# First chunk over 512 tokens beside the loads, spare weight buffers for one output chunk, and small PE steps put later

## What is computed

```python
# first block
h = rmsnorm(x, norm_pre)
pool_u, pool_gate, q, k, v, attn_gate = split(h @ w_in)
pool_out = pool_mixer(pool_u, pool_w, pool_scale) * silu(pool_gate)   # trailing means over 2, 4, 8, 16 tokens
attn_out = sliding_window_attention(q, k, v, sinks) * silu(attn_gate)
x = x + rmsnorm(concat(pool_out, attn_out) @ w_out, norm_post)
# second block
h = rms_norm(x, norm1)            # two attentions and two gates from h @ w_in_2
merged = g_a * (o_a @ w_branch_a) + g_b * (o_b @ w_branch_b)
x = x + merged @ w_out_2
x = x + square(relu(rms_norm(x, norm2) @ w_up)) @ w_down
return rms_norm(x, final_norm)
```

## Time and profile before

| what | value |
|---|---|
| median of 3 runs | 1962.76 us (1958.78 to 1962.78) |
| time of the profiled execution | 1964.96 us |
| its span, first to last instruction | 1963.1 us |
| PE busy, share of the span | 98% |
| DVE, ACT, POOL busy | 48%, 32%, 48% |
| mean granted TensorE clock | 0.995 |
| share of PE in the chain that ended last | 91% |

### The profile page before, as it was taken

The page is one execution under the profiler, slowest core; times in us unless marked ns, Lnnn a source line. Parts: engine busy times, 40 slices in busy tenths (PEclk is TensorE's granted clock), DMA queues, the critical chain, the costliest instruction groups (busy, mean ns, idle before and its releaser), DMA issues.

```text
span 1963.1 us, 27207 instructions
## 1 busy us (share of the span) xinstructions
PE 1924.7 (98%) x9792; PEld 1621.6 (83%) x9792; DVE 946.7 (48%) x1733; ACT 625.2 (32%) x1175; POOL 939.2 (48%) x806
## 2 busy tenths in 40 slices
PE   7999999999999999999999999999999999999998
PEld 6778887888888988888888887878888888888886
DVE  5535664677554544453411116654444444444455
ACT  5025555546444544454300003331111111111133
POOL 3442237622122222112344444486777767777784
PEclk9999999999999999999999999999999999999999
DMA  4311013231111111100111113121121111211103
GB/s 129 103 48 32 29 40 96 81 131 42 36 41 46 26 49 43 44 22 23 33 48 48 48 48 129 54 74 43 43 67 55 51 43 44 71 53 49 54 29 133
DMA packets 147217, 111.98 MB, mean 57 GB/s; under 512 B 11400, under 2 KB 139920, under 8 KB 147104
## 3 DMA queue, kind: packets, MB, share of 16 engines
q1 hardware_dynamic: 134880, 91.77, 16.0%
q10 hardware_dynamic: 12224, 18.70, 3.1%
HBM read 102.00 MB, written 11.59 MB: 58 GB/s over the span
## 4 chain that ended last, share of the span: by engine, by line
PE 91%; DVE 4%; issue 1%; POOL 1%; ACT 1%; DMA 1%; SPq 0%; DVEq 0%; POOLq 0%; ACTq 0%
PE ps L811 7%; PE ps L812 7%; PE ps L813 7%; PE ps L954 7%; PE ps L828 6%; PE ps L829 5%; PE ps L830 5%; PE ps L1171 5%; PE ps L1172 5%; PE ps L1170 5%; PE ps L1131 5%; PE ps L1132 5%; PE ps L1133 5%; PE ps L943 4%; PE ps L929 2%; PE ps L924 2%
## 5 line engine op out<-in xcount | busy, mean ns | idle before, releaser
L667 POOL TENSOR_TENSOR w_hi<-raw,ones 128x512 fp32r<-128x512 f32 x146 | 159.7, 1094 | 797.3 <-PE ps L830 498.3
L2367 DVE TENSOR_TENSOR X<-ps,X 128x1024 f32<-128x1024 f32 x112 | 137.2, 1225 | 205.4 <-PE ps L1172 205.4
L811 PE MATMUL ps<-h_hi,w_hi 128*128 128x512 f32 x544 | 215.1, 395 | 6.0 <-DVE h_lo L1746 3.4
L812 PE MATMUL ps<-h_lo,w_hi 128*128 128x512 f32 x544 | 212.8, 391 | 0.0
L813 PE MATMUL ps<-h_hi,w_lo 128*128 128x512 f32 x544 | 212.7, 391 | 0.0
L671 POOL TENSOR_TENSOR w_lo<-raw,w_hi 128x512 fp32r<-128x512 f32 x146 | 200.1, 1371 | 11.4
L1661 ACT ACTIVATE ps<-ps 128x512 f32<-128x512 f32 x64 | 37.2, 582 | 514.0 <-DVE ps L2344 513.9
L828 PE MATMUL ps<-h_hi,w_hi 128*128 128x512 f32 x480 | 192.0, 400 | 1.2 <-DVE z_swa L1807 1.2
L829 PE MATMUL ps<-h_lo,w_hi 128*128 128x512 f32 x480 | 188.5, 393 | 0.0
L830 PE MATMUL ps<-h_hi,w_lo 128*128 128x512 f32 x480 | 188.0, 392 | 0.0
L1170 PE MATMUL ps<-hid_hi,slot_hi 128*128 128x512 f32 x448 | 174.3, 389 | 0.0
(11 more groups left out here) (333 smaller groups left out, 4292.7 us busy)
## 6 DMA issues: line engine op xcount, KB each, us to landing
raw<-in_w_in SPq DMA_DIRECT2D x116, 256.0 KB, 2.9
down_raw<-in_w_down SPq DMA_DIRECT2D x72, 256.0 KB, 2.7
up<-in_w_up SPq DMA_DIRECT2D x32, 512.0 KB, 4.3
raw<-in_w_out SPq DMA_DIRECT2D x32, 256.0 KB, 2.8
x_in<-in_x SPq DMA_DIRECT2D x8, 512.0 KB, 7.8
raw_b<-in_w_out SPq DMA_DIRECT2D x16, 256.0 KB, 2.9
x_store<-X ACTq DMA_DIRECT2D x8, 512.0 KB, 2.6
bias_fox<-c_rows ACTq DMA_DIRECT2D x8, 512.0 KB, 4.4
```

The lines of the kernel that those rows point to most:

```text
L667: pool.tensor_tensor(w_hi[:, half].rearrange("p k n -> p (k n)"), raw[:, half].rearrange("p k n -> p (k n)"), f32(ones[:, 0:1]).broadcast_ ...
L811: pe.matmul(o, w1, hi[:, k, c], start=first, stop=False)
L812: pe.matmul(o, w1, lo[:, k, c], start=False, stop=False)
```

## The change

It has six parts.

1. SP issues the weights of chunk 0 before x block 3 instead of before block 5.
2. The start goes by halves of the tokens. When blocks 0 to 3 (tokens 0 to 511) are copied, ACT makes the first half of `h_hi` and DVE the first half of `h_lo`, between the copies of blocks 4 to 7; DVE takes over half of these copies. PE computes chunk 0 first over tokens 0 to 511 (`first_step(k, 0)`), of which steps 0 and 1 stand before the turning of block 7, and then over tokens 512 to 1023. The turned blocks go round six banks (2 to 7), since banks 0 and 1 hold chunk 0.
3. The squares go into PSUM (`pair(2)`, `pair(3)`) instead of `sq`, and DVE adds them from there. `mean_square(0)` goes behind the last step of chunk 1, `spread_rms(0)` behind step 3 of chunk 2. DVE lets chunk 1 leave before it pools group 0. `mix(0)` goes behind step 3 of chunk 3, `mix(1)` behind step 3 of chunk 4.
4. `turn_v` goes behind step 3 of the query chunk. In the first attention the wait for the gate chunk's leaving goes behind eight fill steps (`ahead`).
5. `mean_square(2)` goes two half steps later.
6. The second half of the weights of G_OUT2 + 1 is split into the spare buffers `spare_hi` and `spare_lo`, and PE's last four steps read those.

The diff, cut to its core:

```diff
+def x_bank(n):
+    return 2 + n % 6
...
+    spare_hi = z_at("spare_hi", [P, 2, 4, P], F32R, 90)
+    spare_lo = z_at("spare_lo", [P, 2, 4, P], F32R, 92)
...
             for i in range(2, NB):
-                if i == 5:
+                if i == 3:
                     chunk(0, w_in_v, C_POOL, first=True)
...
-            chunks(G_HEADS2 + 3, G_MLP, raw_before=RAW_ELSEWHERE, hi_before=HI_ELSEWHERE)
+            chunks(G_HEADS2 + 3, G_OUT2 + 1, raw_before=RAW_ELSEWHERE, hi_before=HI_ELSEWHERE)
+            for half in range(2):
+                g = G_OUT2 + 1
+                hi, lo = ((w_hi, w_lo), (spare_hi, spare_lo))[half]
+                pool.wait_ge(raw_loaded[half], 16 * (g + 1 - RAW_ELSEWHERE))
+                pool.wait_ge(halves_done, 2 * G_OUT2 + 1)
...
+            chunks(G_OUT2 + 2, G_MLP, raw_before=RAW_ELSEWHERE, hi_before=HI_ELSEWHERE)
...
+                    if 6 <= n < 14:
+                        pe.wait_ge(x_copied, n - 5)
+                    elif n == 14:
+                        pe.wait_ge(x_copied_dve, 1)
+                    elif n == 15:
+                        pe.wait_ge(x_copied, 9)
...
+            def first_step(k, n):
+
+                half, kk, c, o = k // 4, k % 4, slice(n * HALF, (n + 1) * HALF), bank(n)
+                if n:
+                    pe.wait_ge(operand_ready, k + 1)
+                else:
+                    pe.wait_ge(first_ready, k + 1)
+                    if kk == 0:
+                        pe.wait_ge(weights_split, half + 1)
+                pe.matmul(o, w_hi[:, half, kk], h_hi[:, k, c], start=k == 0, stop=False)
+                pe.matmul(o, w_hi[:, half, kk], h_lo[:, k, c], start=False, stop=False)
+                mm = pe.matmul(o, w_lo[:, half, kk], h_hi[:, k, c], start=False, stop=k == KT - 1)
+                if n and kk == 3:
+                    mm.then_inc(halves_done, 1)
+
+            for i in range(NB - 1):
+                turn_x(i)
+            first_step(0, 0)
+            first_step(1, 0)
+            turn_x(NB - 1)
+            for k in range(2, KT):
+                first_step(k, 0)
+            for k in range(KT):
+                first_step(k, 1)
...
-                    if g == 1 and k == 1:
+                    if g == 1 and k == 3:
                         spread_rms(0)
-                if g == 1:
-                    mix(0)
+                    if g == 2 and k == 3:
+                        mix(1)
                 for k in range(KT):
                     k_step(G_POOL + 2 * g + 1, k, 1, 2)
-                    if g == 0 and k == 5:
+                    if g == 1 and k == 3:
+                        mix(0)
+                    if g == 0 and k == KT - 1:
                         mean_square(0)
-                if g:
-                    mix(g)
+            mix(2)
...
-            turn_v(G_V1, 0, 0)
-            chunk(G_SWA, 0)
+            for k in range(KT):
+                k_step(G_SWA, k, 0, 2)
+                if k == 3:
+                    turn_v(G_V1, 0, 0)
...
-                          fill=SWA_Q if j + 1 < PAIRS else SWA_POOL, tail=None if j + 1 < PAIRS else mix_last)
+                          fill=SWA_Q if j + 1 < PAIRS else SWA_POOL, ahead=j == 0, tail=None if j + 1 < PAIRS else mix_last)
...
-                    if f == 0 and k == 3:
+                    if f == 0 and k == 5:
                         mean_square(2)
...
             k_step(G_OUT2, KT - 1, 0, 2, ready=merged_ready, halves=2)
+            pe.wait_ge(weights_split, 2 * (G_OUT2 + 1) + 2)
             for k in range(4, KT):
-                k_step(G_OUT2 + 1, k, 1, 2)
+                mm = half_step(k, 0, 2, spare_hi, spare_lo)
+                mm = half_step(k, 1, 3, spare_hi, spare_lo)
+            mm.then_inc(halves_done, 1)
...
-                act.activation(sq[:, k % 2], src[:, row], ACT.Square).then_inc(squared, 1)
+                act.activation(pair(2 + k % 2), X[:, k], ACT.Square).then_inc(squared, 1)
...
+            for i in range(4):
+                for k in (2 * i, 2 * i + 1):
+                    act.activation(h_hi[:, k, 0:HALF], X[:, k, 0:HALF], ACT.Copy,
+                                   scale=gains[:, 0, k:k + 1]).then_inc(first_hi, 1)
+                copy_x(9 + 2 * i)
...
-                    dve.tensor_tensor(sumsq[:], sumsq[:], sq[:, k % 2], ALU.add).then_inc(summed, 1)
+                    dve.tensor_tensor(sumsq[:], pair(2 + k % 2), sumsq[:], ALU.add).then_inc(summed, 1)
...
+            for i in range(4, NB):
+                dve.wait_ge(x_turned, 2 * i + 1)
+                dve.tensor_copy(X[:, 0:4, i * P:(i + 1) * P],
+                                bank(x_bank(2 * i)).rearrange("p (k n) -> p k n", k=4)).then_inc(x_copied_dve, 1)
+                first_lo(2 * i - 8)
+                first_lo(2 * i - 7)
...
                 leave(G_POOL + 2 * g, VALUES_PAIR[g], u_pad[:, PAD:], 0)
+                if g == 0:
+                    leave(G_POOL + 1, 1, z_gate[:], 0)
```

More of the change, by code:

```diff
@@ L424, in build @@
         x_copied = sem("x_copied")
+        x_copied_dve = sem("x_copied_dve")
+        first_hi = sem("first_hi")
+        first_ready = sem("first_ready")
         operand_hi = sem("operand_hi")
@@ L985, in _, with turn_x @@
             pe.wait_ge(consts_made, 1)
-            for i in range(NB):
+            def turn_x(i):
                 pe.wait_ge(x_loaded[i], 16)
@@ L1299, in operand_hi_k, with square @@
                 act.activation(hi[:, k], src[:, k], ACT.Copy, scale=scale).then_inc(operand_hi, 1)
-            def square(n, k, src, row=None):
-                row = k if row is None else row
-                if KT * n + k >= 2:
-                    act.wait_ge(summed, KT * n + k - 1)
-                act.activation(sq[:, k % 2], src[:, row], ACT.Square).then_inc(squared, 1)
+            def square(k):
+                if k >= 2:
+                    act.wait_ge(summed, k - 1)
+                act.activation(pair(2 + k % 2), X[:, k], ACT.Square).then_inc(squared, 1)
             def inverse_rms(n, readers, between=None):
@@ L1371, in attention, with copy_x @@
                                            ACT.Copy).then_inc(turned_copied, 1)
-            for n in range(2 * NB):
+            def copy_x(n):
                 i, m = n // 2, n % 2
-                if n == 2 * NB - 1:
-                    act.wait_ge(gain_loaded, 16)
-                    act.wait_ge(x_copied, n)
-                    operand_hi_k(0, X, 0)
                 act.wait_ge(x_turned, n + 1)
                 act.activation(X[:, 4 * m:4 * m + 4, i * P:(i + 1) * P],
-                               ps[:, n % 8].rearrange("p (k n) -> p k n", k=4), ACT.Copy).then_inc(x_copied, 1)
-            act.wait_ge(x_copied, 2 * NB)
-            for k in range(1, KT):
-                operand_hi_k(k, X, 0)
+                               bank(x_bank(n)).rearrange("p (k n) -> p k n", k=4), ACT.Copy).then_inc(x_copied, 1)
+            for n in range(8):
+                copy_x(n)
+            act.wait_ge(gain_loaded, 16)
+            act.wait_ge(x_copied, 8)
+            for i in range(4):
[3 more added lines that the diff above has]
+                copy_x(9 + 2 * i)
+            act.wait_ge(x_copied, 12)
+            act.wait_ge(x_copied_dve, 4)
+            for k in range(KT):
+                act.activation(h_hi[:, k, HALF:S], X[:, k, HALF:S], ACT.Copy,
+                               scale=gains[:, 0, k:k + 1]).then_inc(operand_hi, 1)
             load_constants()
@@ L1390, in _ @@
             for k in range(KT):
-                square(0, k, X)
+                square(k)
             inverse_rms(0, None)
@@ L1748, in operand_lo, with add_square @@
                 ins.then_inc(operand_ready, 1)
-            def add_square(n, k):
-                dve.wait_ge(squared, KT * n + k + 1)
+            def add_square(k):
+                dve.wait_ge(squared, k + 1)
                 if k == 0:
-                    dve.tensor_copy(sumsq[:], sq[:, 0]).then_inc(summed, 1)
+                    dve.tensor_copy(sumsq[:], pair(2)).then_inc(summed, 1)
                 else:
-                    dve.wait_ge(summed, KT * n + k)
-                    dve.tensor_tensor(sumsq[:], sumsq[:], sq[:, k % 2], ALU.add).then_inc(summed, 1)
+                    dve.wait_ge(summed, k)
+                    dve.tensor_tensor(sumsq[:], pair(2 + k % 2), sumsq[:], ALU.add).then_inc(summed, 1)
             def inverse_root(n, between=None):
@@ L1921, in _, with first_lo @@
                                      counts[:].rearrange("p g n -> p (g n)")))
+            def first_lo(k):
+                dve.wait_ge(first_hi, k + 1)
+                dve.scalar_tensor_tensor(out=h_lo[:, k, 0:HALF], in0=X[:, k, 0:HALF], scalar=gains[:, 0, k:k + 1],
+                                         in1=f32(h_hi[:, k, 0:HALF]), op0=ALU.mult,
+                                         op1=ALU.subtract).then_inc(first_ready, 1)
+            for i in range(4, NB):
[4 more added lines that the diff above has]
+                first_lo(2 * i - 7)
```

(9 more changed lines are left out.)

17 lines of the change are left out of this document (9 added, 8 removed).

## The result

| | before | after |
|---|---|---|
| median of 4 runs each | 1962.26 us (1958.78 to 1962.78) | 1945.68 us (1945.05 to 1946.88) |
| profiled execution, its span | 1964.96, 1963.1 | 1945.05, 1943.3 |
| mean granted TensorE clock | 0.995 | 0.999 |

The ratio is 0.9917, with a 95% interval of 0.9901 to 0.9933: 16.6 us less, where 15.9 were forecast.

A forecast was written before the change was run, and what follows sets the result against it. PE was taken as the bound, busy for 1924.7 of 1963.1 us. Gains of 3.6 + 4.9 + 1.4 + 1.1 + 0.8 + 4.1 = 15.9 us, against the median 1962.76, gave 1946.9; range 1943.0 to 1952.5.

The forecast's parts named there:

- 1. First chunk: Start of the kernel: with halves of the tokens and earlier weights, chunk 0 ends at 28.9 us; gain 3.6 us.
- 2. Mean square: Chunk 1: squares ready at 38.2 us, before `mean_square` is due at 39.9, so no wait or half clock; gain 4.9 us.
- 3. What follows from it: Inverse root, `spread_rms`, `mix(0)`, `mix(1)` and chunk 3 after the moved mean square: no new waits, gain zero.
- 4 to 6. V's turning, the gate, `mean_square(2)`: PE's waits at V's turning, the gate chunk's leaving and `mean_square(2)` covered by other steps: gains 1.4, 1.1 and 0.8 us.
- 7. Spare buffers: Chunk G_OUT2 + 1: PE's wait for POOL's split goes, and the half clock behind it; gain 2.6 + 1.5 = 4.1 us.
- A: Half clock in the new start, in the first chunk: costs 1.5 to 1.7 us or 3.3, so 1948.5 to 1950.2; chance 0.13.
- B: Start: the operand chain becomes the bound, chunk 0 ends at 31; gain only 11 to 13, 1950 to 1952 us; chance 0.12.
- C: Spare buffers do nothing, the split into them running no earlier: 4.1 us missing, 1951.0 us; chance 0.03.
- D: Slower: the clock falls at the first half steps and stays down through chunks 0 and 1; 1966 us; chance 0.02.

The follow-up runs named there:

- e3: The changed kernel with chunk 0's weights loaded before x block 5 again, their old place; 1947.33 us.
- e2: The changed kernel with the squares back in SBUF instead of PSUM, everything else kept; 1953.92 us.
- e4: The changed kernel with `mean_square(0)` back behind step 5 of chunk 1 and `spread_rms(0)` behind step 1 of chunk 2; 1951.08 us.
- e6: The changed kernel with V's turning, the gate chunk's leaving and `mean_square(2)` back at their old places; 1950.45 us.
- e1: The changed kernel with the spare buffers undone, everything else kept; 1949.27 us.
- e5: The kernel before with the spare buffers alone added; 1959.62 us, ratio 0.9983.
- e8: The kernel before, unchanged, profiled a second time in a single run; 1963.37 us.
- e10: The changed kernel, unchanged, profiled a second time in a single run; 1946.97 us.

## Why the prediction was right, and where its terms were off

The forecast of 1946.9 is 1.2 above the measured median, inside its range, and its likeliest case is the one that came. By its own steps:

**1. First chunk.** 3.6 forecast, 3.9 measured. The layout held: block 3 at 11.16 (11.1 forecast), the first half step at 15.84 (16.3), no wait in chunk 0. PE was done at 27.7 rather than 28.4, and what ended the wait for chunk 1 was POOL, as the text had feared: its hi took 1.93 instead of 1.04, beside DVE's `h_lo`, which has two inputs in SBUF, and the lo ended at 28.5. The step on the loads was right, but no gain of it is shown in the time: e3 stands 1.6 above the changed kernel, within the noise.

**2. Mean square.** 4.9 forecast, 5.2 measured (9.1 at chunk 2's first matmul less 3.9). Squares ready at 37.8 (38.2 forecast), all adds at 1.22 (1.23 taken), due at 39.68. The choice between 1.23 and 1.88 per add carried this term, and e2 shows what the other would have been: a wait of 2.38 and a half clock of 3.3, 5.7 in all, where the sum's lower end had 3.5 and 1.6, 5.1.

**3. What follows from it.** Forecast at nothing, and so it came: no wait at `spread_rms` (46.97) or chunk 3. But the reason given was incomplete. e4 shows that a `mean_square` ahead of the chunk's last steps also holds the weight half, and that the load which is issued 4.4 later by it takes 12.4 us instead of 4.5; at its new place it doesn't. In the kernel before, POOL waited for that load too (7.95, at 72.94), but PE came late enough not to.

**4 to 6. V's turning, the gate, `mean_square(2)`.** 3.3 forecast, 3.5 measured by e6 up to 414 us. The first product with V waits 0.41 where the working left 0.1; still e6 stands 2.5 behind at that product (144.87 against 142.41), which is what terms 4 and 5 had together. In medians e6 costs 4.8, by the ratios 3.9; the intervals don't tell either from 3.5, and how much of it is the clock at 480 us isn't shown.

**7. Spare buffers.** 4.1 forecast, 4.3 between the first two profiles, but 3.6 (e1) and 2.9 (e5) in medians. The step that was mis-sized is "and the half clock with it: 2.6 + 1.5": the 1.5 was read from one execution and taken as certain. It falls due in about half of the executions seen (2 of 4). 2.6 + 0.8 would have been the mean by that share, an estimate from four profiles.

**The sum against the median.** 1964.96 - 15.9 was set off by the 2.2 that the profiled execution lies above its median. e8 and e10 show what such an excess can be made of: half-clock stretches that come or go (1.5 at 489 and 1.5 at 1210 in the profile of before), and a load of up weights that landed 1.7 later there than in e8 (from the second projection's last matmul to the first down product: 34.6 in before, 33.0 in e8, 33.1 in the changed kernel, and 32.9 to 33.2 in the other nine profiles). So the two steps of 1.5 and 1.6 that no term had are no gain of the change: the second is shown by e8, and the first stands at a wait that both kernels have. In medians e1's 3.6 and e6's 4.8 leave 8.2 of the 16.6 for terms 1 and 2, against 8.5 forecast, though each of these medians is uncertain by some us. The mechanism of each term is borne out; that the sum came within 1.2 of the median is partly luck, since the single terms, and the correction of 2.2 for the profiled execution, aren't known that closely.

**The rivals.** A came in part: a half clock in the start shows in e3, and in e5 and e8, whose start is the old one, but not in the changed kernel's two profiles. What the text held against it, that chunk 0 of the kernel before ran at the full pace, was true of one execution: in e8, the same kernel, the first matmuls of chunk 0 stand 0.43 apart (0.50 at 22 to 24 us) behind the wait of 2.74. Its cost in e3 was 1.6 at the end of chunk 0, as given, and 0.9 at chunk 1. e4's profile shows another form, a clock that rises late: 1.2 at chunk 1. So the chance of 0.13 was no overstatement. The Trainium skill, page TensorE: Matmul & The Clock Gate, section Part 4: PE-mode transpose, would have it come always, since transposes don't engage the full clock. Here blocks 0 to 2 were turned at half pace and blocks 3 to 7 at full (8 in 1.09 us), and before block 3 PE had done nothing but transposes, so the trace doesn't bear that out for these float32 ones. B did not come: DVE was ready in time for each half step. C is ruled out by e1 and e5. D did not come: every fall of the clock seen in the 12 profiles before the last 30 us ended within 8 us. The text counted two such stretches in the profile of before; there is a third, at 490 to 493 us, behind the wait of 1.31.

## What to carry to other kernels

Where a wait stands between a chain on another engine and PE, look first at the form of that chain's instructions: moving one operand of DVE's adds from SBUF to PSUM took a third off the median add, and the same move freed POOL, which was splitting the next weights beside it. A mark placed before a chunk's last steps holds that chunk's buffers for as long as it lasts; follow the release through the splitting engine to the load queue before costing it at nothing. And of a single profile take the waits as they are, but count the clock behind a wait of some 1 to 3 us by the share of executions in which it falls, or profile the same kernel twice.

## What the runs showed of the hardware that was not expected

- The granted clock behind one and the same wait of 2.58 us was 0.50 in two executions and 1.00 in two, with the same work on both sides. Behind a wait of 1.31 it fell in 5 of 12. A stretch cost 1.5 to 1.7 us where PE was the bound, and 3.3 in e2 and in e8, where it took in the one-column matmuls as well (from the start of `mean_square` to `spread_rms` 10.6, against 7.3 in the changed kernel).
- The full clock came with PE at nothing but 128x128 float32 transposes: 8 of them took 1.84 to 1.94 us at first and 1.09 later, and the change came ahead of block 3 in the changed kernel's first profile, and only at about 15.5 us in e4's.
- The spread between executions isn't explained. The kernel before took 1957.3 to 1964.9 us in 13 runs with a mean clock of 0.994 to 0.997, the changed kernel 1945.05 to 1946.97 in 5 with 0.997 to 0.999. Half-clock stretches that come and go would do part of that, but the mean clock doesn't show it: two runs of e4 took 1951.09 and 1951.06 us with 0.995 and 0.999.
- DVE's adds with both inputs in SBUF and POOL's lo splits slow each other down: 1875 against 1225 ns, and 2.13 to 2.17 against 1.3 us (e2). POOL's hi, with 1.04 us alone, took 1.93 beside DVE's two-input `h_lo`.
